# Attention of a two-layer trunk on eight cores: by tiles of frames, with the other tiles' queries and two tiles' output products between its steps

## The reference

```python
# w_qkv: 2048 -> 32 query heads + 4 key heads + 4 value heads, of 64
q, k, v = qkv_proj(h, w_qkv, b_qkv)
# a query chunk of 64 frames reads its own chunk and the two before it: 192 keys
s = einsum('bnqhgd,bnkhd->bnhgqk', q, k) * HEAD_DIM ** -0.5 + bias   # relative position
p = softmax(concatenate([s, sink], -1))[..., :-1]                    # one learned sink a head
o = einsum('bnhgqk,bnkhd->bnqhgd', p, v)
x = x + g1 * (o.reshape(B, S, 2048) @ w_o + b_o)                     # output products
h = modulate(rms_norm(x, norm_ffn), sh2, sc2)                        # then the gated network
x = x + g2 * ((silu(h @ w_g) * (h @ w_u)) @ w_down)
```

## Time and profile before

| what | value |
|---|---|
| time before, median of 3 runs | 3705.44 us (3302.58 to 3746.4) |
| the profiled execution's own time | 3301.68 us |
| its span, first to last instruction (slowest core, 5) | 3300.6 us |
| spans of the eight cores | 3281.4 to 3300.6 us |
| TensorE busy | 3030.2 us, 92% of the span |
| VectorE, ScalarE, GpSimd busy | 1234.4, 738.3, 290.2 us |
| mean granted TensorE clock of core 5 | 0.956 |

### The profile page before, as it was taken

How to read it: one execution, slowest core, us unless ns; L and a number is a source line. 1 busy time by engine, 2 the same in 40 slices (tenths; PEclk the granted TensorE clock), 3 DMA queues, 4 the chain that set the end, 5 groups by cost and what they waited for, 6 DMA issues and landing times.

```text
span 3300.6 us, 58445 instructions; the slowest of 8 cores (3281.4 to 3300.6 us)
## 1 busy us (share of the span) xinstructions
PE 3030.2 (92%) x23566; PEld 1862.0 (56%) x23566; DVE 1234.4 (37%) x2763; ACT 738.3 (22%) x1710; POOL 290.2 (9%) x474
## 2 busy tenths in 40 slices
PE   2399997879999999999999989898999999999997
PEld 0155554445556565565565555455666666666664
DVE  0356766442321413113412647733231222223416
ACT  1412225551000000000002547655100000000013
POOL 0000000000000000000001025410000000000000
PEclk8599998989999999999999999789999999999999
DMA  9877764625756476573667122133584435443442
GB/s 221 152 114 127 131 116 104 132 39 100 131 96 131 75 135 115 99 137 72 116 119 131 30 53 49 30 63 60 101 137 70 77 66 84 69 77 56 86 77 106
DMA packets 73592, 320.57 MB, mean 97 GB/s; under 512 B 11952, under 2 KB 28176, under 8 KB 45808
## 3 DMA queue, kind: packets, MB, share of 16 engines
q0 software_dynamic: 49440, 283.78, 49.2%
q1 hardware_dynamic: 23888, 33.06, 3.5%
HBM read 590.55 MB, written 10.70 MB: 182 GB/s over the span
## 4 chain that ended last, share of the span: by engine, by line
PE 82%; DMA 6%; DVE 5%; ACT 3%; issue 3%; another core or an unknown queue 1%; SPq 0%; DVEq 0%; ACTq 0%; POOL 0%; POOLq 0%
PE ps L230 81%; DMA RING<-wmod 2%; ACT SCR L233 2%; DMA X<-xT 1%; DMA RING<-wgu 1%; DMA RING<-wpw 1%; PE ps L1394 1%; ACT RING L233 1%; DVE SCR L544 1%; ACT HBraw L233 1%; DVE UBraw L1400 0%; DVE X L457 0%; SPq L225 0%; DVE X L952 0%
## 5 line engine op out<-in xcount | busy, mean ns | idle before, releaser
L230 PE MATMUL ps<-HBraw,RING 128*128 128x384 bf16 (+4 forms) x10848 | 1767.0, 325 | 39.1 <-ACT SCR L233 21.2
L230 PEld LDWEIGHTS ps<-HBraw,RING 128*128 128x128 bf16 x10848 | 1051.7, 98 | 722.6 <-issue 58.3
L230 PE MATMUL ps<-UBraw,RING 128*128 128x384 bf16 (+3 forms) x6016 | 964.8, 319 | 29.5 <-ACT UBraw L233 19.8
L230 PEld LDWEIGHTS ps<-UBraw,RING 128*128 128x128 bf16 x6016 | 572.4, 99 | 395.7 <-issue 65.3
L627 DVE TENSOR_TENSOR UBraw<-ps,SCR 128x384 bf16<-128x384 f32 (+2 forms) x264 | 144.3, 547 | 1190.7 <-PE ps L230 1171.2
L233 ACT ACTIVATE SCR<-ps 128x384 f32<-128x384 f32 (+2 forms) x264 | 127.1, 482 | 1772.2 <-PE ps L230 1772.1
L466 DVE SCALAR_TENSOR_TENSOR X<-ps,MOD,X 128x384 f32<-128x384 f32 (+2 forms) x960 | 388.8, 446 | 290.5 <-PE ps L230 289.1
L230 PE MATMUL ps<-SCT,RING 128*128 128x3 bf16 x3072 | 91.4, 165 | 61.8 <-DMA RING<-wmod 52.0
L225 POOL DMA_DIRECT2D RING<-wgu x88 | 46.6, 529 | 1073.0 <-PE ps L230 1069.7
L225 POOL DMA_DIRECT2D RING<-wmod x96 | 52.0, 542 | 941.4 <-PE ps L230 932.6
L230 PEld LDWEIGHTS ps<-SCT,RING 128*128 128x128 bf16 x3072 | 89.8, 97 | 72.2 <-issue 64.4
(11 more groups left out here) (96 smaller groups left out, 1213.3 us busy)
## 6 DMA issues: line engine op xcount, KB each, us to landing
RING<-wmod POOLq DMA_DIRECT2D x96, 1024.0 KB, 12.4
RING<-wgu POOLq DMA_DIRECT2D x88, 1024.0 KB, 9.2
RING<-wdn POOLq DMA_DIRECT2D x80, 512.0 KB, 8.9
RING<-wpw POOLq DMA_DIRECT2D x24, 1024.0 KB, 16.5
X<-xT SPq DMA_DIRECT2D x4, 2368.0 KB, 54.6
RING<-wqkv POOLq DMA_DIRECT2D x16, 512.0 KB, 6.5
X<-xT SPq DMA_DIRECT2D x32, 192.0 KB, 2.6
RING<-wo POOLq DMA_DIRECT2D x5, 1024.0 KB, 9.5
```

The source lines that it names most:

```text
L230: return PE.emit(nc.tensor.matmul(out, lhsT=lhsT, rhs=rhs, start=start, stop=stop, **kw))
```

## The change

The kernel after makes the attention go tile by tile. Its 66 items are the chunks of tile 0 for groups 3, 2, 1, 0, then those of tile 1 for the four groups, then the two samples, then those of tile 2: 13 stretches instead of 5, each with a bias table of its own, loaded two stretches ahead. What is moved with it:

- Ahead of the attention stand the queries of tile 0 for all groups (`q_first`), not those of group 3 for all tiles. The queries of tiles 1 and 2 for all groups are in `q_fill`.
- `wo_fill(0)` and `wo_fill(1)` give all 16 output blocks of tiles 0 and 1 between the steps; behind the barrier only tile 2 is left.
- The weights of the queries are streamed twice and those of the output three times, once for each use.
- `fill` gives 2.6 us a step in the first eight stretches and 2.2 us after.
- VectorE evicts the transposes (`turned_out(i-3)`) right behind `biased(i)`, ahead of `inverse(i-1)` and `least(i)`.
- Behind the barrier each output block of tile 2 is followed by up to three squares of the tiles that are waiting (`wo_ready`), so their norm is made beside it.

```diff
+                for b in (6, 7, 4, 5, 2, 3):
+                    whalves(f"q0_{b}", wqkv[b])
+                plan.append(("attn", 32, None, (5, NHALF)))
+                for b in (0, 1):
+                    whalves(f"q0_{b}", wqkv[b])
                 for b in (6, 7, 4, 5, 2, 3, 0, 1):
-                    whalves(f"q_{b}", wqkv[b])
-                plan.insert([p[0] for p in plan].index("q_4b"), ("attn", 32, None, (5, NHALF)))
-                for b in range(3):
-                    whalves(f"wo_{b}", wo[b])
+                    whalves(f"q1_{b}", wqkv[b])
+                for t in range(2):
+                    for b in range(8):
+                        whalves(f"wo{t}_{b}", wo[b])
+                for b in range(2):
+                    whalves(f"wo2_{b}", wo[b])
                 zone[0] = (0, NHALF)
-                for b in range(3, 8):
-                    wblock(f"wo_{b}", wo[b], KC)
+                for b in range(2, 8):
+                    wblock(f"wo2_{b}", wo[b], KC)
...
-        items = [(g, qc) for g in (3, 2, 1, 0) for qc in range(16)]
-        items[56:56] = [("s", 0), ("s", 1)]
+        stretches = [(g, t) for t in range(2) for g in (3, 2, 1, 0)] + [("s", 2)] + [(g, 2) for g in (3, 2, 1, 0)]
...
+        def q_first(g):
+
+            xlo, zn = L1T[0]
+            for b in (2 * g, 2 * g + 1):
+                rows, ids = use_halves(f"q0_{b}")
+                for n in (2 * b, 2 * b + 1):
+                    bk = kv_bank()
+                    for k, (slot, kx) in enumerate(rows):
+                        mm(PS[bk][:, 0:zn], slot[:, kx, 128 * (n % 2):128 * (n % 2) + 128], HB[:, k, 32 + xlo:32 + xlo + zn],
+                           k == 0, k == KC - 1)
+                    q_out(n, 0, bk, PE.tick())
+                    after_group(1.5)
+                for i in ids:
+                    ring_release(i)
...
+        def wo_fill(t):
+            xlo, zn = L1T[t]
+            while t not in att_t:
+                yield None
+            PE.wait(*att_t[t])
+            for b in range(8):
+                rows, ids = use_halves(f"wo{t}_{b}")
+                for n in (2 * b, 2 * b + 1):
                     bk = fill_bank()
-                    PE.wait(*att_t[t])
-                    for k in wo_products(two[n // 2][0], n, t, PS[bk]):
+                    for k in wo_products(rows, n, t, PS[bk]):
                         if k % 4 == 3:
                             yield 4 * zn / 2400
                     pending.append((bk, wo_out, (n, t, bk, PE.tick())))
+                for i in ids:
+                    ring_release(i, False)
...
-        filler[0] = itertools.chain(q_fill(2), q_fill(1), q_fill(0), wo_fill())
+        filler[0] = itertools.chain(q_fill(3), q_fill(2), q_fill(1), q_fill(0), wo_fill(0), wo_fill(1))
...
-            fill(4.0 if i < 3 else 1.75)
+            fill(2.6 if stretch_of[min(i, nit - 1)] < 8 else 2.2)
             if new:
                 biased(i)
+            if back3:
+                turned_out(i - 3)
...
-            if back3:
-                turned_out(i - 3)
...
+            xlo, zn = L1T[2]
             for n in (2 * b, 2 * b + 1):
-                for t in range(3):
-                    wo_group(rows, n, t)
+                bk = 3 + pk % 5
+                pk += 1
+                PE.wait(bfree[bk])
+                for k in wo_products(rows, n, 2, PS[bk]):
+                    pass
+                if last:
+                    norm3.square(*last.popleft())
+                last.append((n, 2, epilogue_bias(1, n, xlo, zn, bk, PE.tick())))
+                after_group(1.3)
+                for _ in range(3):
+                    if wo_ready:
+                        norm3.square(*wo_ready.popleft())
+                after_group(1.3)
```

## The result

The changed kernel takes 1.0158 times the time of the kernel before (interval 1.0138 to 1.0178): 3356.34 us at the median of 5 runs, the profiled execution 3354.89, against 3305.18 at the median of the kernel before in the same series. Forecast were 3286.

The account below looks back on a forecast made before the run. TensorE's chain was taken as the bound, with 69.5 us lost to idling and low clock; after the change 53.9 would remain, a gain of 15.6 from 3301.7, giving 3286 us, range 3256 to 3316.

Parts of the forecast that it names:

- So TensorE sets the pace: Filled attention steps: about 3.9 to 4.0 us of TensorE work against VectorE's 3.12; small waits fall from 5.1 to 3.
- neither is on the path, so it costs nothing: Filled steps: evicting the transposes earlier delays the division by one copy, under 0.7 us, at no cost.
- nothing more waits for it: GpSimd's queue: the next division stands behind a transfer waiting for a release already due, so no further wait.
- Waits for output weights: Tile 0's output blocks between the steps: 7.0 us each instead of 5.4, 13 us in all, bounds 0 and 20.
- The landing: Output weights for tile 0: a pair of half slots lands 7.4 us after its issue.
- The rival of a stream that is too slow: Weight stream becomes the bound: 65 us more, 3351 us, deciding from a landing time of about 9.4; chance 0.12.
- The start: From tile 0's queries to the first steps: TensorE loses 8.3 us against 7.6 before, bounds 4.8 and 12.
- The hole's work: Steps from 45, unfilled before the change: matmuls now stand in each step up to 62, so 37.5 us lost go.
- The bare end: Last attention steps without fill, some 19 us with a low clock in its last part; 13.6 us lost, barrier included.
- issued two stretches ahead, 16 us or more: Eight more bias tables: loaded early enough for no wait, or 1 to 2 us at one or two borders.
- Behind the barrier: Tile 2's 16 output blocks with squares beside them: TensorE waits 12 us for ScalarE, bounds 0 to 30.
- The gate's wait: Norm ahead of the second gate block: TensorE idle 4 us in place of 16.9, bounds 3 to 12.

Follow-up runs that it names:

- late additions: Changed kernel with VectorE's addition of a filled-in output product moved behind the step's minimum: ratio 1.0022 to the kernel before, profiled 3316.93 us.
- both causes out: Changed kernel with additions behind the minimum and one resident block of output weights for tiles 0 and 1 (wrong results): ratio 0.9974, profiled 3295.75 us.

## Why the prediction was wrong

**The step that failed** is "So TensorE sets the pace", with the sentence ahead of it: "less on ScalarE, whose added work in a step is one and a third evictions". I added up each engine's work. The added eviction has a follower on VectorE, the addition, which the part on the steps never names, and by its place it ties the two engines into a ring with the exponentials. The same step said of the copy "neither is on the path, so it costs nothing": 8.5 us. In figures, steps 44 to 62 were to take 18 x (1.28 + 2.2) = 63 us; they took 95.5, and 75.6 without the ring.

**A second term was mis-sized through the first.** From a block's last matmul to the issue of its refill I took 1.2 us, and "nothing more waits for it" looked only at what is queued behind the transfer. What is queued ahead of it, a division that waits for VectorE, made it 9.8 us in the place shown, 5.3 on average, and 2.4 with late additions. Waits for output weights were 18.5 us on average against 13, and 14.1 with late additions. The landing I took for that of the whole pair, 7.4 us. Of the pair only the first transfer is waited for; over the same 64 blocks it took 6.9 us on average, while the whole pair took 8.8 in the place shown. So the size was about right, in part by luck. The rival of a stream that is too slow decided from 9.4 us. Only where two pairs were asked for 3 us apart did the awaited landing come near that (9.2 and 10.6 us on core 6), and all the streaming of output weights is worth 19.5 us, not 65 more than forecast. The time landed near this rival's 3351 by another mechanism. The Trainium skill, "DMA: Bandwidth & Descriptors", section "Anatomy of one DMA — SWDGE (gpsimd) path", gives 3.2 us for a half slot by its fit; the median of the 36 on core 6 is 7.2 us, so here too the trace decides.

**The start** was sized rightly and made up otherwise: 8.3 us told, and 7.6 found (two waits for query weights of 3.48 and 3.44 us where I had 5.2 and 2, and 0.72 ahead of the first scores). Beside it stand 3.65 us in four gaps of the values' groups of tile 0, against 1.83 and 0.29 in the kernel before, which neither side of my sum had. From the first keys to the first scores it is 75.4 us against 67.1; the 5.9 us that the kernel before lost there came behind its first scores.

**What held.** The hole's work did move: steps 0 to 32 ran at 3.9 us, TensorE idle 1 us in 136. The bare end, told as some 19 us with a low clock in its last part, is 23.8 us from the end of the last fill at 2249.5 to the first product of tile 2 at 2273.3, at a clock of 0.50 in its last 12; with late additions, where the ring no longer reaches into it, it is 19.1. No stretch border of the changed kernel waited for a bias table, but in part by luck: "issued two stretches ahead, 16 us or more" is wrong behind the samples, where it is three steps. At 5 us each, with the ring, they cover the table; at 3.5 us they do not on most cores. Behind the barrier TensorE waited 8.9 us for ScalarE, against 12, and 3.6 for output weights at 2292.94, which I had not. The gate's wait was named rightly and sized too small: 6.8 us idle in three pieces, and a clock of 0.81 in the 14 us behind it, against 4 in all.

**The account.** From 3286 to 3354.9 is 69 us. The ring is 40, the weights 6.5 more than counted (19.5 against 13), the rest of the stage 10 (my steps come to 242 us, with the small waits I gave them to 245, and with both causes out it is 255.5; 3 of it is VectorE, full at 3.64 us a step where I had 3.48), the gate 5, the start 1, and behind the barrier 3 less for ScalarE and 3.6 more for weights. Some 7 us lie ahead of the stage, which begins at 1869.55 on the slowest core and at 1862.40 before: code that the change does not touch, on a core that may differ from run to run (the mean of the eight cores moves by 1.7). That makes 70, one more than there is; the parts are not known better than that. With both causes out the change gives 0.26%: the new start, the rest of the stage, the bare end and the squares behind the barrier take back most of the 69.5 us that it could win.

## What to carry to other kernels

When a step gets one more operation, write down its whole chain over all engines, and look what stands ahead of each of its members in its engine's order; if the chain comes back to the next step's first operation, its length is the period, and no sum of busy times will show it. Put such a follower behind the last operation that the other engine waits for. An operation that the change makes frequent mostly has a few instances in the trace of before: measure the period of those steps.

A transfer that is issued from a computing engine's queue is only as prompt as that engine's slowest input: check what is ahead of it, not only behind.

A load that is asked for some stretches of work ahead has as much time as the shortest of these stretches leaves it: count in steps, and again with the steps as short as you want to make them.

## What the runs showed of the hardware

With late additions an addition of 128 x 384 takes 1.33 us (1377 ns is the mean of 16), against 0.56 in the changed kernel. What differs is what runs beside it on GpSimd; the kernel with late additions, core 6:

```profile
2174.71 1.47 POOL L1428 TENSOR_TENSOR SCR<-RING,RD 128x768 bf16<-128x768 f32 x1 [1.76 <-DVE RD L1422]
...
2178.35 1.46 POOL L1428 TENSOR_TENSOR PB<-RING,RD 128x768 bf16<-128x768 f32 x1 [0.40 <-DVE RD L1422]
```

Each addition (2175.26, 2178.90) starts inside a division and ends 0.41 us after it. The Trainium skill, "SBUF — State Buffer", section "Who interferes with whom", says that a VectorE instruction with both inputs in SBUF contends with a GpSimd instruction that reads SBUF. The ports that they share are by it an exclusive lock, and the order of issue decides who waits; the trace agrees. The same kernel with the copy in its old place, core 6, where the addition starts later in the division:

```profile
2187.59 1.47 POOL L1428 TENSOR_TENSOR PB<-RING,RD 128x768 bf16<-128x768 f32 x1 [2.74 <-DVE RD L1422]
2188.28 1.19 DVE L1302 TENSOR_TENSOR X<-X,HBraw 128x384 f32<-128x384 f32 x1
```

It starts 0.69 us into the division and not 0.55, takes 1.19 us and not 1.33, and ends the same 0.41 us after it. `biased`, which reads PSUM and SBUF, takes 0.95 us also inside a division (changed kernel, `biased` at 2196.87, division from 2196.32 to 2197.78). No run here moved the addition out of the division, so what this costs late additions (up to 0.8 us a step, where VectorE sets the pace) was not tried.
